# First weight piece of each mixture split in two halves, and half of the broadcast of dense expert weights moved behind its products

## The reference, cut to what matters

```python
def grouped_moe(h, router_w, router_b, w_gate, w_up, w_down):
    scores = jax.nn.sigmoid((t @ router_w).astype(jnp.float32))
    sel = scores + router_b.astype(jnp.float32)
    ...
    combine = jnp.einsum('nk,nke->ne', top_w, jax.nn.one_hot(top_idx, N_EXPERTS, dtype=jnp.float32))
    for e in range(N_EXPERTS):
        he = jax.nn.silu(t @ w_gate[e]) * (t @ w_up[e])
        y = y + combine[:, e:e + 1] * (he @ w_down[e]).astype(jnp.float32)
```

## Time and profile before

| | us |
|---|---|
| median of 3 runs | 2256.76 (2254.9 to 2262.32) |
| the profiled execution, its own time | 2256.28 |
| its span in the profile | 2254.5 |
| PE busy | 2159.2 (96%) |
| DVE busy | 1407.1 (62%) |
| ACT busy | 1029.8 (46%) |
| mean granted TensorE clock | 0.986 of full speed |

### The profile page before, as it was taken

One profiled execution on the slowest core, in us unless ns is written; L12 is line 12 of the kernel. 1 busy time (PEld: TensorE's weight loads), 2 busy tenths in 40 slices (PEclk: granted clock), 3 DMA queues, 4 the chain that ended last, 5 costly groups with the idle time before them and its releaser, 6 DMA issues.

```text
span 2254.5 us, 32931 instructions
## 1 busy us (share of the span) xinstructions
PE 2159.2 (96%) x14046; PEld 1775.2 (79%) x14046; DVE 1407.1 (62%) x1458; ACT 1029.8 (46%) x1155; POOL 80.8 (4%) x138
## 2 busy tenths in 40 slices
PE   6998899999999899999999999889999999999999
PEld 4777777678787777687788897778888888888887
DVE  5766745689775743489766565466566576635655
ACT  4344422367545423277644445335444444435443
POOL 2040000000000000000000000000000000020000
PEclk9999899999999899999999999999999999999999
DMA  9872969999670858999655550006554555433553
GB/s 344 327 233 97 307 248 366 365 336 358 218 266 1 274 189 315 332 339 357 211 187 187 187 161 26 4 24 211 197 187 168 185 181 203 146 86 127 191 187 112
DMA packets 267313, 475.61 MB, mean 211 GB/s; under 512 B 9424, under 2 KB 151824, under 8 KB 262944
## 3 DMA queue, kind: packets, MB, share of 16 engines
q1 hardware_dynamic: 256128, 431.81, 55.1%
q0 software_dynamic: 11040, 41.70, 5.5%
HBM read 471.33 MB, written 2.14 MB: 210 GB/s over the span
## 4 chain that ended last, share of the span: by engine, by line
PE 86%; DVE 6%; ACT 4%; DMA 2%; issue 1%; POOL 0%; ACTq 0%; DVEq 0%; SPq 0%; POOLq 0%
PE psum L1074 14%; PE psum L1076 7%; PE psum L1091 4%; PE psum L1093 3%; PE psum L1092 3%; PE psum L1042 3%; PE psum L1044 3%; PE psum L1043 3%; PE psum L1411 3%; PE psum L1366 2%; PE psum L1367 2%; PE psum L1368 2%; PE psum L1523 2%; PE psum L1525 2%; PE psum L1524 2%; DVE w_lo L2806 2%
## 5 line engine op out<-in xcount | busy, mean ns | idle before, releaser
L2806 DVE TENSOR_TENSOR w_lo<-ring,w_hi 128x2048 fp32r<-128x2048 f32 x267 | 609.9, 2289 | 289.0 <-ACT w_hi L2157 282.9
L2157 ACT ACTIVATE w_hi<-ring 128x2048 fp32r<-128x2048 f32 x267 | 510.8, 1915 | 361.7 <-PE psum L1093 119.9
L1074 PE MATMUL psum<-h_both,w_hi 128*128 128x512 f32 x1408 | 498.6, 398 | 1.7 <-DVE h_both L3511 1.3
L1076 PE MATMUL psum<-h_both,w_lo 128*128 128x256 f32 x1408 | 395.2, 281 | 0.0
L1074 PEld LDWEIGHTS psum<-h_both,w_hi 128*128 128x128 f32 x1408 | 264.4, 188 | 67.5 <-issue 1.7
L1076 PEld LDWEIGHTS psum<-h_both,w_lo 128*128 128x128 f32 x1408 | 265.9, 189 | 1.4
L2806 DVE TENSOR_TENSOR w_lo<-pool,w_hi 128x2048 fp32r<-128x2048 f32 x70 | 160.4, 2291 | 106.1 <-ACT w_hi L2157 105.6
L2157 ACT ACTIVATE w_hi<-pool 128x2048 fp32r<-128x2048 f32 x70 | 134.1, 1915 | 163.6 <-DMA pool<-in_exp_w_up 62.1
L2179 ACT ACTIVATE pool<-psum 128x512 f32<-128x512 f32 x88 | 52.6, 598 | 260.4 <-PE psum L1076 260.4
L1042 PE MATMUL psum<-w_hi,h_both 128*128 128x512 f32 (+1 forms) x352 | 141.3, 402 | 5.5 <-DVE w_lo L2806 2.8
L1366 PE MATMUL psum<-h_both,w_hi 128*128 128x256 f32 x480 | 139.1, 290 | 1.1 <-DVE w_lo L2806 1.1
(11 more groups left out here) (479 smaller groups left out, 3795.8 us busy)
## 6 DMA issues: line engine op xcount, KB each, us to landing
ring<-in_ffn_pre_w_in SPq DMA_DIRECT2D x44, 1024.0 KB, 5.1
ring<-in_ffn_post_w_in SPq DMA_DIRECT2D x44, 1024.0 KB, 5.1
pool<-in_exp_w_up SPq DMA_DIRECT2D x40, 1024.0 KB, 8.3
ring<-in_exp_w_gate SPq DMA_DIRECT2D x36, 1024.0 KB, 7.5
ring<-in_exp_w_down SPq DMA_DIRECT2D x30, 1024.0 KB, 7.6
ring<-in_ada_w SPq DMA_DIRECT2D x24, 1024.0 KB, 6.9
ring<-in_ffn_pre_w_out SPq DMA_DIRECT2D x22, 1024.0 KB, 4.9
ring<-in_ffn_post_w_out SPq DMA_DIRECT2D x22, 1024.0 KB, 4.9
```

Of the source, the lines that this page charges most:

```text
L1074: pe.matmul(o.rearrange("p (s n) -> p s n", s=2), wh[:, k, fs], h_both[:, :, k, :], start=k == 0, stop=False, skip_group_check=True)
L1076: m = pe.matmul(o[:, 0:T], wl[:, k, fs], h_hi[:, k, :], start=False, stop=k == KD - 1, skip_group_check=True)
L2157: act.activation(w_hi[:, (s["split"] + r) % 3, :], piece(s["pieces"][r]), ACT.Copy)\
L2806: dve.tensor_tensor(w_lo[:, slot, :], piece(s["pieces"][r]), w_hi[:, slot, :].bitcast(F32), ALU.subtract).then_inc(sem("w_lo"), 1)
```

## The change

1. SP loads the first piece of each mixture (the gate piece of step 0) as two DMAs of 512 KB, k 0 to 3 with the semaphore `first_half_in`, k 4 to 7 with the slot's own.
2. ACT rounds it in two halves of 1024 columns, DVE subtracts it in two. `first_half_hi` says that the first half is rounded. (It takes over the job of `rotated` as well, and `landed0` that of `stored`, at other places of the program.)
3. PE starts on the first half; the order of its 32 products with `w_hi` is now by k first and by output half second, with a wait before k = 4.
4. PE spreads only the first two rows before the piece (`comb_rows(0)`) and the other two behind its products (`comb_rows(1)`).
5. DVE's copy of bank 7, with its wait and its `side_dve`, leaves the router's end and goes behind the split of piece 3 and the third `ada_parts`, ahead of `product(0)`.

```diff
+                    elif n == m["first"]:
+                        src, dst = expert(kind, layer, 4 * group[0], 0), piece(n).rearrange("p (k n) -> p k n", k=KD)
+                        sp.dma_start(dst[:, 0:4, :], src[:, 0:4, :]).then_inc(sem("first_half_in"), 16)
+                        sp.dma_start(dst[:, 4:8, :], src[:, 4:8, :]).then_inc(sem(f"landed{PL.pieces[n]['slot']}"), 16)
...
-                for e in range(4):
-                    m = pe.matmul(bank(6 + e // 2)[:, T * (e % 2):T * (e % 2) + T],
-                                  bc(ident[0:NE, e:e + 1], [NE, P]), comb_t, start=True, stop=True)
-                    if e % 2:
-                        m.then_inc(sem("comb_ps"), 1)
+                comb_rows(0)
+
+            def comb_rows(half):
+
+                for e in range(2):
+                    m = pe.matmul(bank(6 + half)[:, T * e:T * e + T], bc(ident[0:NE, 2 * half + e:2 * half + e + 1], [NE, P]), comb_t,
+                                  start=True, stop=True)
+                m.then_inc(sem("comb_ps"), 1)
...
                     if n == 0:
-                        for f in range(2):
-                            for k in range(KD):
+                        pe.wait_ge(sem("first_half_hi"), 1 + layer + 1)
+                        for k in range(KD):
+                            if k == 4:
+                                pe.wait_ge(sem("w_split_hi"), U0 + 1)
+                            for f in range(2):
...
                         m.then_inc(sem("w_used"), 1)
+                        comb_rows(1)
                         return
...
-                for n in range(3):
+                act.wait_ge(sem("w_used"), U0 - 2)
+                act.wait_ge(sem("first_half_in"), 16 + 16 * layer)
+                act.activation(w_hi[:, U0 % 3, 0:1024], piece(m_["first"])[:, 0:1024], ACT.Copy).then_inc(sem("first_half_hi"), 1)
+                act.wait_ge(sem(f"landed{PL.pieces[m_['first']]['slot']}"), PL.pieces[m_["first"]]["landed"])
+                act.activation(w_hi[:, U0 % 3, 1024:2048], piece(m_["first"])[:, 1024:2048], ACT.Copy).then_inc(sem("w_split_hi"), 1)
+                for n in range(1, 3):
                     split(n)
...
-                dve.wait_ge(sem("comb_ps"), 2 * layer + 2)
-                dve.tensor_copy(flat(comb_b[:, 2:4, :]), bank(7)).then_inc(sem("side_dve"), 1)
-
...
-                for n in range(4):
+                dve.wait_ge(sem("first_half_hi"), 1 + layer + 1)
+                dve.tensor_tensor(w_lo[:, U0 % 3, 0:1024], piece(m_["first"])[:, 0:1024], w_hi[:, U0 % 3, 0:1024].bitcast(F32), ALU.subtract)
+                dve.wait_ge(sem("w_split_hi"), U0 + 1)
+                dve.tensor_tensor(w_lo[:, U0 % 3, 1024:2048], piece(m_["first"])[:, 1024:2048],
+                                  w_hi[:, U0 % 3, 1024:2048].bitcast(F32), ALU.subtract).then_inc(sem("w_lo"), 1)
+                for n in range(1, 4):
                     split(n)
-                    if n > 0:
-                        ada_parts(0, n - 1)
+                    ada_parts(0, n - 1)
+                dve.wait_ge(sem("comb_ps"), 2 * layer + 2)
+                dve.tensor_copy(flat(comb_b[:, 2:4, :]), bank(7)).then_inc(sem("side_dve"), 1)
                 product(0)
```

More of the change, by code:

```diff
@@ L756, in _ @@
             sp.wait_ge(sem("x_new"), 10)
-            sp.dma_start(out.rearrange("a (t p) d -> p (a t) d", p=P), x[:, :, :]).then_inc(sem("stored"), 16)
-            sp.wait_ge(sem("stored"), 16)
+            sp.dma_start(out.rearrange("a (t p) d -> p (a t) d", p=P), x[:, :, :]).then_inc(sem("landed0"), 16)
+            sp.wait_ge(sem("landed0"), 16 * PL.loads[0] + 16)
         @block.gpsimd
@@ L807, in _ @@
             pl.wait_ge(sem("mem_ps"), 2)
-            pl.wait_ge(sem("rotated"), 1)
+            pl.wait_ge(sem("first_half_hi"), 1)
             for h in range(8):
@@ L1236, in beside_even @@
                         pe.wait_ge(sem(e[0]), e[1])
-                    pe.wait_ge(sem("rotated"), 1)
+                    pe.wait_ge(sem("first_half_hi"), 1)
                     even_turned("ret_qk", (0, 1) if n == 9 else (2, 3))
@@ L1343, in wide_up @@
                     n = at[kind, c, 0]
-                    if n == 0:
-                        pe.wait_ge(sem("w_split_hi"), U0 + 1)
-                    else:
+                    if n > 0:
                         pe.wait_ge(sem("w_lo"), U0 + n + 1)
@@ L2980, in even_first @@
                     rotate(1)
-                    dve.memset(tiny[:, 160:161], 0.0).then_inc(sem("rotated"), 1)
+                    dve.memset(tiny[:, 160:161], 0.0).then_inc(sem("first_half_hi"), 1)
                 if c == 5:
```

## The result

The median is 2266.13 us (6 runs, 2263.37 to 2266.74) against 2255.83 for the kernel before (6 runs, 2253.26 to 2262.32) on the same chip. The ratio is 1.0034, 95% interval 1.0021 to 1.0048: slower by 0.34%. The forecast was 2258.6, +2.3; the result is +7.7 by the ratio (the two medians of six runs lie 10.3 apart). So the change costs 4 to 8 us, about 6. The sign was right, the size was not.

What follows compares the result with a forecast made beforehand. PE, busy for 96% of the span, was taken to wait for ScalarE's rounding of the first gate piece. Layer 0's +1.80 and layer 1's +0.48 gave +2.28 us on 2256.28: 2258.6, range 2255.0 to 2262.5.

Steps and rivals of the forecast that it cites:

- The new wait drops the clock: Rival, chance 0.03: layer 0's 1.32 us wait before L1474 starts a 13.6 us low spell; +8.3, 2264.6 us.
- Load in halves, cost 0: First piece's load: one more issue delays later pieces by at most 0.53 us, covered by 1 us; cost 0.
- Rounding in halves: First piece on ACT: a half takes 1.02 us, so PE starts 0.89 us earlier in both layers.
- What the clock makes of 0.89: First piece: with the clock rising at the same moments, the 0.89 us earlier start gains 0.50 in each layer.
- Half of the spread moved: Two spread products behind the first piece cost PE 0.98 us; its arrival at L1474 moves +0.48 in each layer.
- DVE's copy moved: Before L1474, PE waits for the late copy: +1.80 in layer 0, 1.32 of it waiting; +0.48 in layer 1.
- What the clock does behind the wait: Behind layer 0's wait before L1474: no fall counted in the sum; a dropped clock was only a rival, chance 0.03.
- The row at 400 us: Profile row cited against a dropped clock: a wait of 1.5 us at 400 us left the clock at 1.00.
- The sum: Whole kernel: 1.80 in layer 0 plus 0.48 in layer 1, +2.28 us on 2256.28, giving 2258.6.
- The range: Whole kernel: 2255.0 to 2262.5 us, widened for scatter of runs and taking in the middle of the late clock.

Runs made afterwards that it cites:

- halves with late copy: The full change, but with all four spread products in front of the first piece and the copy still late: 2264.01 us, 1.0029 against the kernel before.
- The filled wait of both layers: The full change, with PE repeating L1479's transposes during the wait, five times over in layer 0, twice in layer 1: 2265.18 us, 1.0030 against the kernel before.
- that of layer 0: The full change, with L1479's four transposes done four times over in layer 0 alone: 2260.04 us, 1.0013 against the kernel before.

## Why the prediction was wrong

It failed at the clock behind the new wait. I gave the rival "The new wait drops the clock" 0.03, priced it as one long spell, and put nothing for it in the sum. The traces have a spell of 3.4 us there, worth about 1.6, in a sum whose other terms were 0.9 too small. By the steps of the prediction:

- *Load in halves, cost 0.* Right. Both halves are issued in 0.40 and 0.38 us, the first lands 3.5 us after its issue, piece 1 at 10.7 us behind the order (before 10.6), and PE waits neither for it nor before k = 4. The Trainium skill, "DMA: Bandwidth & Descriptors", section "Anatomy of one DMA", has its formula for a DMA on GpSimd's queue. Taken as an estimate for these loads on SyncE's queue, it would have the half 1.2 us ahead of the whole; here it is 5.2 against 3.5, 1.7.
- *Rounding in halves.* Right: 1.05 us for 1.02, PE 0.97 earlier for 0.89. By the Trainium skill, "VectorE: DVE Perf Modes", section "The TRN2 errata — SBUF-src ops pay a fixed extra latency per instruction", a ScalarE copy of 1024 columns is, as an estimate, (224 + 1024) / 1.2 GHz = 1.04 us; the trace agrees with 1.05.
- *What the clock makes of 0.89.* Wrong, but not costly. I kept the clock's rise where it was and took 0.50. It moved with the start: to 12.3 us behind the order from 13.3 in layer 0, to 10.8 from 11.7 in layer 1. So the full 0.97 and 0.89 were won.
- *Half of the spread moved.* 1.12 us in place of 0.98. PE starts the transposes into bank 6 at 251.05 - 228.63 = 22.42, before at 22.16: +0.26, and +0.37 in layer 1 (21.79 for 21.42). Predicted were +0.48 in each, and +0.09 with the rise moving along, which is the case that came; the rest is the dearer pair and a slower first product of piece 1.
- *DVE's copy moved.* The mechanism, the place and the layer were right. The size: the transposes into bank 7 come at 24.75, +2.15 for +1.80, with 1.73 us of waiting for 1.32. The copy itself is 0.4 later than I had it. The third modulation load, on POOL's queue, is issued at 15.95 (before 15.78) and takes 6.8 us in place of 6.6, so VectorE waits 1.16 us for it where it waited 0.84. In layer 1 I let the copy end ahead of PE; PE waits 0.47 for it, +1.00 for +0.48.
- *What the clock does behind the wait.* The step that failed. I argued from a wait of 1.5 us at 400 us that left the clock up, and took a fall to be the long one of 13.6 us or none. It was one of 3.4 us: 1.5 us more, +1.6 at the first down product (44.80 against 41.06, of which 2.15 stood at the transposes). In five traces with the copy late behind halves (this one, the second and third of the full change, halves with late copy, late copy in layer 0 only) layer 0 waited 1.4 to 2.8 us, and in all five the clock fell behind the wait. It stayed up at this place behind idles of 1.0 us and less, and where the wait was filled.
- The row at 400 us was no freak: each of the 18 traces has such idles elsewhere, with the clock at 1.00 throughout. In the kernel before:

```profile
586.62 0.50 PE L1554 MATMUL psum<-w_hi,hid_hi 128*128 128x512 f32 x1 [1.41 <-DVE hid_lo L3228]
...
598.54 2.16 PE L995 MATMUL psum<-pool,x 128*128 128x128 f32 x17 [1.69 <-DVE pool L2617]
```

```profile
570.00:740.00 170.00, 157.91 (x999) 134.84 (x998) 112.29 (x123) 90.95 (x112) 4.77 (x9) 1.00 0.44 150
```

- So the length of an idle doesn't decide by itself. What is particular to the place is what follows the wait: two transposes and then twelve products of 4 columns each, 1.4 to 1.7 us of them (L1486). Whether that makes the difference no run tested.
- *The sum.* Forecast 1.80 + 0.48 = 2.28. The profiled execution has 2.15 + 1.6 in layer 0 and 1.06 in layer 1, 4.8. Of the 2.5 missing, 1.6 is the fall, 0.35 and 0.58 the later copy in the two layers. The three ratios give 7.7, 6.5 and 4.3 us.
- *The range* assumed that the medians of two kernels are known to about 3 us. It reached 2262.5; with the fall priced at its small size, as a likely case, it would have gone to 2264 or so, which the first median, 2266.13, still misses and the other two, 2263.71 and 2260.82, don't.

Shown by runs: the loss needs the halves and the late copy together (1.0029 with both and no moved products, 1.0005 and 0.9984 to 0.9989 with one), it sits in layer 0 (1.0020 against 1.0002), and it goes when the copy stands one instruction earlier (1.0006). Why the late copy alone cost so little isn't shown; its one trace had an early load. Seen in the traces only: that the fall makes some 1.6 us of the loss; the stretch from order to order points the same way. The filled wait of both layers didn't lower the total (1.0030), and that of layer 0 did so by less than the measurement can tell (1.0013 against 1.0019). What lies between 4.8 us and the 6 of the three measurements stays open; it may be nothing but scatter.

## What to carry to other kernels

A copy that another engine waits for belongs ahead of the instruction that waits for a DMA, not behind it: the copy takes on that wait, and so does everyone behind its semaphore. When an edit lets TensorE start earlier, look for the next semaphore that was only just in time; here 1 us won at the start was lost at a place where PE had gone by without waiting. And where an edit opens an idle of TensorE, let the sum have a case with a short spell at the lower clock behind it: here 1.4 us and more ahead of small products were followed by one six times out of six, while idles of up to 1.7 us elsewhere, ahead of products of 128 to 512 columns, were not. A counterexample at another place doesn't rule it out.

## What the hardware showed

- Behind idles of 1.4, 1.65, 1.7 (twice), 2.0 and 2.8 us ahead of the transposes into bank 7, the clock fell to 0.50 between 0.9 and 2.1 us after the end of the wait, while PE was at work again, and came back 3.4 to 6.8 us later. Behind idles of 0.4 to 1.0 us at the same place it didn't, nor behind 1.5 us at 400 us, 1.41 at 586.6 and 1.69 at 598.5, so the idle alone doesn't decide. The Trainium skill, "TensorE: Matmul & The Clock Gate", section "What's actually happening", has two levels of the clock in its table; the windows here agree, with 0.50 and 1.00 wherever a window lies within one spell.
- The same program differs from itself by up to 18 us (2249.9 to 2268.17 in 35 executions), and where the low spells fall differs from trace to trace. Three measurements of one kernel gave 1.0034, 1.0029 and 1.0019.
- ScalarE's and VectorE's halves overlap in the profile: the second half on ACT begins 0.94 us after the first, though each takes 1.05; on VectorE it is 1.14 after the first, which takes 1.23. Two halves cost 1.99 us of ACT, one whole 1.91.
